# Scan decays from a split sum, and cross attention's products in three rounded parts

## What is computed

```python
# scan: chunks of 128 tokens, 16 heads of 64, 2 groups, state 128
a_cs = jnp.cumsum(ac, axis=-1)
seg = a_cs[..., :, None] - a_cs[..., None, :]
decay = jnp.exp(jnp.where(causal, seg, -jnp.inf))
cb = jnp.einsum('bclgn,bcsgn->bcgls', cm, bm)
y_diag = jnp.einsum('bcgkls,bcsgkp->bclgkp', cb[:, :, :, None] * decay, xc)
decay_to_end = jnp.exp(a_cs[..., -1:] - a_cs)
chunk_decay = jnp.exp(a_cs[..., -1])
def step(h, inp):
    st, dec = inp
    return h * dec[..., None, None] + st, h
y_off = jnp.einsum('bclgn,bcgkpn,bcgkl->bclgkp', cm, prev, jnp.exp(a_cs))

# cross attention: 4 heads of 256, 512 queries, 256 memory tokens
s = jnp.einsum('blhd,bmhd->bhlm', q, k) * (XA_HEAD_DIM ** -0.5)
p = jax.nn.softmax(s, axis=-1)
o = jnp.einsum('bhlm,bmhd->blhd', p, v)
```

## Time and profile before

| | before |
|---|---|
| median of 3 runs | 2520.03 us (2519.97 to 2525.08) |
| the profiled execution's own time | 2524.29 us |
| its span in the profile | 2522.5 us |
| granted clock of TensorE, mean | 0.996 |
| DMA, mean over the span | 100 GB/s |

### The profile page before, as it was taken

How to read it: one execution, slowest core, us unless ns; L and a number is a source line. 1 busy time by engine, 2 the same in 40 slices (tenths; PEclk the granted TensorE clock), 3 DMA queues, 4 the chain that set the end, 5 groups by cost and what they waited for, 6 DMA issues and landing times.

```text
span 2522.5 us, 38409 instructions
## 1 busy us (share of the span) xinstructions
PE 2471.1 (98%) x15181; PEld 2144.2 (85%) x15181; DVE 1699.1 (67%) x3249; ACT 1294.5 (51%) x2558; POOL 404.4 (16%) x476
## 2 busy tenths in 40 slices
PE   7999999999999999999999999999999999999998
PEld 6876677899988978778897999889898887999888
DVE  5476977688863499997774988535635744987533
ACT  4365554367742435564654687424534453677422
POOL 2233342200000156553000100000000100100000
PEclk9999999999999999999999999999999999999999
DMA  9532234434443233223421333332321442333332
GB/s 285 136 93 71 63 101 121 132 99 126 118 126 98 80 101 94 58 67 95 131 84 51 92 111 108 96 96 82 93 76 34 134 126 59 85 111 107 93 99 86
DMA packets 455092, 253.29 MB, mean 100 GB/s; under 512 B 16458, under 2 KB 449310, under 8 KB 454911
## 3 DMA queue, kind: packets, MB, share of 16 engines
q1 hardware_dynamic: 451615, 243.18, 33.7%
q0 software_dynamic: 3152, 7.59, 1.2%
q10 hardware_dynamic: 144, 0.07, 0.0%
HBM read 247.99 MB, written 2.80 MB: 99 GB/s over the span
## 4 chain that ended last, share of the span: by engine, by line
PE 84%; DVE 10%; ACT 3%; issue 2%; DMA 1%; SPq 0%; POOL 0%; DVEq 0%; ACTq 0%; POOLq 0%
PE ps L1134 15%; PE ps L1136 15%; PE ps L1142 15%; PE ps L1199 4%; PE ps L1201 4%; PE ps L1204 4%; PE ps L1049 4%; PE ps L1051 4%; PE ps L1047 4%; PE ps L1375 2%; PE ps L1232 1%; DVE ps L3034 1%; PE ps L1229 1%; PE ps L1227 1%; PE ps L1720 1%
## 5 line engine op out<-in xcount | busy, mean ns | idle before, releaser
L1950 ACT ACTIVATE wh<-w_f 128x512 fp32r<-128x512 f32 (+2 forms) x621 | 351.1, 614 | 337.7 <-PE ps L1142 158.1
L2914 DVE TENSOR_TENSOR w_r<-w_f,wh 128x512 fp32r<-128x512 f32 (+1 forms) x459 | 295.9, 688 | 334.1 <-ACT wh L1950 333.6
L1134 PE MATMUL ps<-XH,wh 128*128 128x512 f32 (+1 forms) x1136 | 458.0, 403 | 4.4 <-ACT wh L1950 3.5
L1136 PE MATMUL ps<-XL,wh 128*128 128x512 f32 (+2 forms) x1016 | 398.0, 392 | 0.2 <-DVE XL L3434 0.2
L1142 PE MATMUL ps<-XH,w_r 128*128 128x512 f32 (+2 forms) x1160 | 309.2, 390 | 1.1 <-DVE w_r L2914 0.8
L1136 PE MATMUL ps<-arena_r,wh 128*128 128x512 f32 (+1 forms) x808 | 297.1, 373 | 0.1
L4213 POOL TENSOR_TENSOR w_r<-w_f,wh 128x256 fp32r<-128x256 f32 (+1 forms) x314 | 236.1, 782 | 352.2 <-ACT wh L1950 352.2
L1134 PEld LDWEIGHTS ps<-XH,wh 128*128 128x128 f32 (+1 forms) x1136 | 211.9, 186 | 69.2 <-issue 16.0
L1142 PEld LDWEIGHTS ps<-XH,w_r 128*128 128x128 f32 (+2 forms) x1160 | 215.5, 186 | 51.2 <-DVE w_r L2914 3.2
L1136 PEld LDWEIGHTS ps<-XL,wh 128*128 128x128 f32 (+2 forms) x1016 | 189.5, 186 | 42.8 <-issue 1.7
L1134 PE MATMUL ps<-arena_r,wh 128*128 128x512 f32 (+1 forms) x568 | 210.6, 379 | 0.8 <-ACT wh L1950 0.8
(11 more groups left out here) (499 smaller groups left out, 5913.4 us busy)
## 6 DMA issues: line engine op xcount, KB each, us to landing
w_f<-in_mlp_w SPq DMA_DIRECT2D x126, 512.0 KB, 4.0
w_f<-in_w_ff SPq DMA_DIRECT2D x63, 512.0 KB, 4.1
w_f<-in_w_in SPq DMA_DIRECT2D x49, 512.0 KB, 3.9
w_f<-in_ada_w SPq DMA_DIRECT2D x35, 512.0 KB, 4.0
w_f<-in_even_w_in SPq DMA_DIRECT2D x35, 512.0 KB, 3.8
w_f<-in_odd_w_in SPq DMA_DIRECT2D x23, 512.0 KB, 3.7
w_f<-in_even_w_out SPq DMA_DIRECT2D x16, 512.0 KB, 3.9
w_f<-in_xa_w_v SPq DMA_DIRECT2D x16, 512.0 KB, 3.3
```

Source lines behind the costliest of these rows:

```text
L1134: e.matmul(b, hi[:, k, :], xh, start=u.first and k == 0, stop=False)
L1136: e.matmul(b, hi[:, k, :], xl, start=False, stop=False)
L1950: e.activation(high_flat(u)[:, s], flat(u, 0)[:, s], ACT.Copy).then_inc(act.sem, act.up("high", u.n, i))
L2914: e.tensor_tensor(low[:, s], raw_[:, s], high[:, s], ALU.subtract).then_inc(dve.sem, dve.up("low", u.n, i))
```

## The change

In the **scan**, the running sums of all 16 heads of a chunk are made in the projections' stage, turned so that heads lie on partitions: three copies of the step widths (`adt_thrice`), four float32 products, a rounded copy of two thirds of the 48 rows and a remainder in the last third, and GpSimd spreads each chunk to 48 x 512 with the other heads set to zero (`decay_split`). A step's seg is then one rounded product of 48 rows by 512 columns. The mask add and its table go: ScalarE takes Relu(a_cs - seg) in four instructions out of PSUM and then one exponential of 128x512 with scale -1; the causal mask is a 0/1 product on C·B that GpSimd does. DE comes from one exponential for all chunks. The old state is multiplied by DE on GpSimd (not in chunk 0, where it is zero). The scan's tap slots change from 3 each (2 in step 14) to 4 in steps 0 to 9 and 3 in 10 to 12; the root's from 4 + 4 to 0 + 3. The first four gated inputs move from step 14 to step 13, and come after that step's outputs.

In **cross attention**, queries, keys, weights and values are split: ScalarE makes the high parts (of keys and values two instructions of 128x1024 each), VectorE the low parts of queries and weights, GpSimd those of keys and values (one instruction of 128x2048 each). Scores and values become three rounded products. The bank of the turned weights and that of a query unit are now freed by VectorE. Some buffers move in the arena.

```diff
         tap_slots |= {("xbc", m): 1 for m in XBC_ORDER[8:XBC_FIRST]} | {("xbc end",): 6}
-        tap_slots |= {("scan", st): 3 if st < 14 else 2 if st == 14 else 0 for st in STEPS}
-        tap_slots |= {("root", 0): 4, ("root", 1): 4}
+        tap_slots |= {("scan", st): 4 if st < 10 else 3 if st < 13 else 0 for st in STEPS}
+        tap_slots |= {("root", 0): 0, ("root", 1): 3}
...
# TensorE
+            for c in range(NT):
+                last = e.matmul(b[0:DECAY_ROWS, c * P:(c + 1) * P],
+                                adt_thrice[:, c * DECAY_ROWS:(c + 1) * DECAY_ROWS],
+                                upper, start=True, stop=True)
...
             def scan_decay(st):
...
-                for j in range(4):
-                    hd = st * 4 + j
-                    last = e.matmul(b[:, j * P:(j + 1) * P], adt[:, hd:hd + 1].to_broadcast([P, P]), upper,
-                                    start=True, stop=True)
+                w.wait_ge(pool, "decay blocks", c)
+                e.matmul(b[:, :], group_pick[0:DECAY_ROWS, q4:q4 + 1].to_broadcast([DECAY_ROWS, P]), decay_split[c],
+                         start=True, stop=True).then_inc(pe.sem, pe.up("seg", st))
...
                 def cross_begin(hd, qt):
-                        last = e.matmul(b[:, 0:MEM], qT[:, 2 * hd + j, qt * P:(qt + 1) * P], kT[:, 2 * hd + j, :],
-                                        start=j == 0, stop=j == 1)
+                        e.matmul(b[:, 0:MEM], q_high[:, m, ts], k_high[:, m, :], start=j == 0, stop=False)
+                        e.matmul(b[:, 0:MEM], q_high[:, m, ts], k_low[:, m, :], start=False, stop=False)
+                        last = e.matmul(b[:, 0:MEM], q_low[:, m, ts], k_high[:, m, :], start=False, stop=j == 1)
...
                 def cross_weigh(hd):
+                    w.wait_ge(dve, "xpt", li, hd, NT - 1)
+                    w.wait_ge(act, "values high", li)
+                    w.wait_ge(pool, "values low", li)
...
-                            last = e.matmul(b[:, :], vv[:, kt, m * P:(m + 1) * P], pt[:, kt, :], start=kt == 0, stop=kt == 1)
+                            e.matmul(b[:, :], v_high[:, kt, c], high[:, kt, :], start=kt == 0, stop=False)
+                            e.matmul(b[:, :], v_high[:, kt, c], low[:, kt, :], start=False, stop=False)
+                            last = e.matmul(b[:, :], v_low[:, kt, c], high[:, kt, :], start=False, stop=kt == 1)
...
# ScalarE, scan_decay: after E1
-                w.wait_ge(dve, "seg", st)
-                w.wait_ge(dve, "nacs")
+                    w.wait_ge(pe, "y", st - 2)
...
-                    e.activation(DEC[:, j, :], DEC[:, j, :], ACT.Exp, bias=nacs[:, hd:hd + 1]).then_inc(
-                        act.sem, act.up("dec", st))
+                    e.activation(DEC[:, j, :], bb[:, j, :], ACT.Relu, bias=acs[:, hd:hd + 1], scale=-1.0).then_inc(
+                        act.sem, act.up("fall", st))
+                att4.free(act, "seg", st)
+                w.wait_ge(act, "fall", st)
+                e.activation(DEC, DEC, ACT.Exp, scale=-1.0).then_inc(act.sem, act.up("dec", st))
...
# VectorE: scan_mask is gone, and in scan_state
-                    e.tensor_tensor(half[par], half[par], de[:, g * 4:(g + 1) * 4, par].unsqueeze(2).to_broadcast([P, 4, DH]),
-                                    ALU.mult).then_inc(dve.sem, dve.up())
...
+                def weights_low(hd, qt):
+                    high, low = (a[:, :, qt * P:(qt + 1) * P] for a in pt_ring[li].of(hd))
+                    w.wait_ge(act, "xpt", li, hd, qt)
+                    e.tensor_tensor(low, att4.of("xt", li, hd, qt)[:, 0:MEM].rearrange("p (a b) -> p a b", a=2),
+                                    high.bitcast(F32), ALU.subtract).then_inc(dve.sem, dve.up("xpt", li, hd, qt))
+                    att4.free(dve, "xt", li, hd, qt)
...
                 for i, tile in enumerate(tiles):
                     cross_begin(*tile)
+                    if i > 1:
+                        weights_low(*tiles[i - 2])
...
# GpSimd, in the loop over st, after CE of st + 1
+                if q4 == 0:
+                    scan_groups(c, 1)
+                elif c < NT - 1 and q4 == 2:
+                    scan_groups(c + 1, 0)
...
+                elif q4 % 2 and 0 < c < NT - 1:
+                    scan_fade(c, q4 // 2)
...
+            def scan_groups(c, g):
+                w.wait_ge(act, "cb", c, g)
+                e.tensor_tensor(CB[:, g, :], CB[:, g, :], upper, ALU.mult).then_inc(pool.sem, pool.up("cb", c, g))
...
+            def scan_fade(c, g):
+                w.wait_ge(pe, "y", 4 * c + 2 * g + 1)
+                w.wait_ge(dve, "state", c - 1, g)
...
+            def values_low(li):
+                w.wait_ge(act, "values high", li)
+                e.tensor_tensor(v_low, vv, v_high.bitcast(F32), ALU.subtract).then_inc(pool.sem, pool.up("values low", li))
```

More of the change, by code:

```diff
@@ L90 @@
 NEAR = 8
+O_KEYS = 12416
+O_PT_LOW = ARENA - 1024 - 16
 ADA_AFTER = {1: 0, 4: 1, 7: 2, 10: 3}
@@ L112, in shape_constants @@
     upper = (i[:, None] <= i[None, :]).astype(np.float32)
-    seg_mask = np.where(i[:, None] <= i[None, :], 0.0, NEG).astype(np.float32)
+    picks = np.zeros((P, PICKS), np.float32)
+    rows = np.concatenate([i[:SSM_HEADS], i[2 * SSM_HEADS:3 * SSM_HEADS]])
+    for j in range(4):
+        picks[rows, j] = rows % 4 == j
+        picks[rows, 4 + j] = rows % SSM_HEADS // 4 == j
     again = np.tile((np.arange(S) % GLA_C != 0).astype(np.float32), (P, 1))
@@ L2102, in evacuate @@
                     lin.free(act, *u.out)
+                elif name in cross_queries:
+                    w.wait_ge(pe, "unit", u.n)
+                    copy(q_high[:, m, :], b, "query high", name[1], m)
                 elif name in TURNED:
@@ L2689, in layer_biases, with keys_high, values_high @@
                 return biases
+            def keys_high(li):
+                for h in range(2):
+                    ks = slice(h * QUARTER, (h + 1) * QUARTER)
+                    w.wait_ge(act, ("mk", li), KC - 1)
+                    copy(k_high[:, ks, :], kT[:, ks, :], "keys high", li)
+            def values_high(li):
+                for t in range(2):
+                    w.wait_ge(act, "stored", ("mv", li), KC - 1)
+                    copy(v_high[:, t, :], vv[:, t, :], "values high", li)
             def cross_attention(stage):
@@ L3064, in evacuate @@
                                            op0=ALU.mult, op1=ALU.add).then_inc(dve.sem, dve.up("yout", m))
+                    lin.free(dve, *u.out)
+                elif name in cross_queries:
+                    w.wait_ge(act, "query high", name[1], m)
+                    e.tensor_tensor(q_low[:, m, :], b[:, :], q_high[:, m, :].bitcast(F32), ALU.subtract).then_inc(
+                        dve.sem, dve.up(name, m))
                     lin.free(dve, *u.out)
@@ L3704, in vector_program @@
                     conv_taps("gv", i)
[L3706 to L3719 removed]
+                if i == 7:
+                    b, low = att4.of("decay rows"), slice(2 * SSM_HEADS, DECAY_ROWS)
+                    w.wait_ge(act, "decay high")
+                    e.tensor_tensor(decay_rows[low, :], b[low, :], decay_rows[low, :].bitcast(F32), ALU.subtract).then_inc(
+                        dve.sem, dve.up("decay low"))
+                    att4.free(dve, "decay rows")
             def scan_decay(st):
@@ L3755, in scan_state @@
             def scan_state(c, g):
-                de = DE.rearrange("p (g two) -> p g two", two=2)
                 b = att4.of("state", c, g)
@@ L3965, in cross_attention @@
                         cross_low((i - 6) // 4)
+                for tile in tiles[-2:]:
+                    weights_low(*tile)
                 cross_low(HEADS - 1)
@@ L4378, in scan_inputs @@
                         pool.sem, pool.up("xw", c, g))
+            def scan_fade(c, g):
+                de = DE[:, c * SSM_HEADS:(c + 1) * SSM_HEADS].rearrange("p (g two) -> p g two", two=2)
+                w.wait_ge(act, "de")
+                w.wait_ge(pe, "y", 4 * c + 2 * g + 1)
+                w.wait_ge(dve, "state", c - 1, g)
+                for par in range(2):
+                    half = pair(ST)[:, g * 4:(g + 1) * 4, par, par * DH:(par + 1) * DH]
+                    e.tensor_tensor(half, half, de[:, g * 4:(g + 1) * 4, par].unsqueeze(2).to_broadcast([P, 4, DH]),
+                                    ALU.mult).then_inc(pool.sem, pool.up("fade", c, g))
             for u in plans["ev xbc"]:
```

146 lines of the change are left out of this document (90 added, 56 removed).

## The result

The changed kernel took 2530.45 us (median of 8 runs, 2528.93 to 2533.28); the kernel before, run beside it, 2526.11 (8 runs, 2519.97 to 2530.99). The ratio is 1.0027, with a 95% interval of 1.0015 to 1.0039: 4 to 10 us slower, where 14.3 us faster was forecast.

A forecast was written before the change was run, and what follows sets the result against it. TensorE, busy 98% of the span, was taken as the bound. Scan -8.1 us and cross attention -6.2 summed to -14.3, from a median of 2520.0 to 2505.7 us; range 2498 to 2517.

The forecast's parts named there:

- VectorE sets the scan: Rival: in the scan VectorE needs 5.59 us a step, so 1.8 us is won instead of 8.6; 2512.5 us, chance 0.14.
- The waits of the values for the weights' low part: Cross attention: TensorE waits for VectorE's subtraction before the values; 2 us a layer, 4 in all (0 to 14).
- 13 x 0.66 = 8.6 us: Scan: one rounded product of 0.23 us replaces sums of 0.89, saving 0.66 a step in 13 steps from seg(3).
- I take that wait as unchanged (0 to 3 us): Scan: ScalarE's evacuation of a finished tile holds up a step, 1.17 us at y(14) before; no change counted.
- -0.4 (0 to 1.4): End of the short convolution: two masks and copies less let VectorE start earlier, saving 0.4 us.
- -11.2: Cross attention: rounded products save 5.8 us on the scores of 32 tiles and 5.4 on the values of eight heads.
- Where a query unit ... lies between, nothing shows: at i = 10.: Cross attention: a query unit of 5.5 us covers the wait for the weights' subtraction, so it costs nothing there.
- I take 1.0, for layer 1 only: Layer 1's cross attention: tile 0's scaling may wait out GpSimd's long instruction on SBUF ports; 1.0 us, range nothing to 3.
- Cross attention gives it back: Rival: the weights' subtraction shows at most tiles, 10 us instead of 5; 2510.7 to 2512 us, chance 0.15.
- its one rival: Scan's loop: ScalarE's chain sets the step, 6.6 us or more; at 7.2 us a step +13, 2533 us; chance 0.04.

The follow-up runs named there:

- e10: Changed kernel with each step's rounded product for the decay sums issued twice; undisturbed steps went from 5.12 to 5.34 and from 5.25 to 5.48 us.
- e9: Changed kernel; in the scan ScalarE evacuates a finished tile behind the next step's decays and GpSimd adds it behind CE; ratio to before 1.0004.
- e7: Changed kernel; in the scan only ScalarE's evacuation of a finished tile moves behind the next step's decays; ratio to before 1.0039.
- e1: Kernel before plus the scan's edits alone, with the old cross attention; ratio to before 1.0006.
- e2: Kernel before plus cross attention's edits alone, with the old scan; ratio to before 1.0040.
- e8: Changed kernel; layer 1's values' parts early, weights' low part behind the query unit, ScalarE's (not GpSimd's) tile-end work late; ratio to before 1.0007.
- e4: Changed kernel with VectorE making the weights' low part of tile i-2 behind the query unit, not ahead of it; ratio to before 1.0023.
- e5: Changed kernel with cross attention's values as float32 products again, scores still three rounded ones; ratio to before 0.9978.
- e3: Changed kernel with layer 1's high and low parts of the values made ahead of the last query unit before cross attention; ratio to before 1.0019.
- e6: Changed kernel with cross attention's scores as float32 products again, values still three rounded ones; ratio to before 1.0035.
- e12: Changed kernel with the old three taps a scan step (2 in step 14), not four in the first ten; ratio to before 1.0030.
- e11: Changed kernel with float32 values, split scores, and ScalarE's and GpSimd's tile-end work in the scan moved later; 2511.99 us, ratio to before 0.9948.

## Why the prediction was wrong, point by point

**What held.** The step of the scan: 5.12 to 5.25 us, 5.1 forecast. VectorE keeps up in the undisturbed steps, about as narrowly as forecast (0.15 us a step to spare): from 1048 to 1080 it stood idle three times, 1.25 us in six steps. C and B's product had a median of 0.71 us, so the rival "VectorE sets the scan" is out. Four Relus took 1.13 to 1.16 us, no table load came, GpSimd was in time in the undisturbed steps. In layer 2 the same lock (a scaling of 4.14 us at 2069.35) cost nothing, as a query unit lay over it. The waits of the values for the weights' low part, set at 4 us for both layers, were 3.7.

**"13 x 0.66 = 8.6 us".** Mis-sized. From the four rounded products ahead of the sums to y it was 0.92 + 0.98 us before and is 1.00 + 0.42: 0.48 saved a step, not 0.66. e10 shows that the product itself was rightly priced; what was missing is 0.09 us ahead of the sums and 0.09 more ahead of y, where weights are loaded late. 13 x 0.18 = 2.3 us.

**"I take that wait as unchanged (0 to 3 us)"**, of a tile's end. It became 2.10 and 1.94 us at two steps, 4.0 in all against 1.2. That is beyond the 3 us of its own bound. ScalarE's and GpSimd's queues had no slack for the work at a tile's end; e9 shows it, and e7 that one queue is not enough. Together: 13 x 0.48 = 6.2 saved, 4.0 lost and 1.2 won back at y(14) make 3.4; measured at full clock, y(2) to y(15) of e1, it is 3.7. The clock's 1.4 us stand against 1.3 in the kernel before and change little in the 4.2 us of the table.

**"-0.4 (0 to 1.4)"**, for an earlier end of the short convolution. It did not show: TensorE's wait there ended at 1041.98, at 1040.75 before, and at 1041.48 in e2, which has the old scan. No run tells what of this is drift.

**"-11.2" for the products of cross attention.** Nearly right. Where no wait disturbs it, a tile with its turning went from 1.08 to 0.94 us and a head's values from 3.43 to 2.72: 32 x 0.14 + 8 x 0.71 = 10.2 us. Between the turnings (14 tiles, 3 heads) that is 4.1 us a layer. But TensorE's busy time fell there by 2.7 us in layer 1 (48.4 to 45.7, e8) and 2.8 in layer 2 (53.6 to 50.7, after), as each wait costs more than its row: the last product ahead of it is not overlapped, and the first behind it starts slowly. In e8's layer 1 that makes 4.1 - 2.7 = 1.4 us for six waits, in layer 2 after 1.3 for five: some 0.24 us a wait, an estimate from these sums. The forecast had no such term.

**"Where a query unit ... lies between, nothing shows: at i = 10."** The step that failed most. I asked what the subtraction waits for and how late that makes the values, and not what stands behind it in VectorE's queue: the roundings, the low part of that very query unit, the next maximum. Three waits of 2.2 to 2.3 us stand behind it (L1754 for L3136 twice, for L2764 once in layer 1); e4 takes 4.8 us back between the turnings, and e5, without the subtraction, has one wait of 0.45.

**"I take 1.0, for layer 1 only"**, of the lock. The mechanism was right, the size wrong: 5.4 us by e3 between the turnings of layer 1, above the 3 that I gave as the end. VectorE's 4.15 us were seen; that three tiles then come late one after the other, and that a clock falls behind them, was not.

**The clock.** Nowhere in the sum. In layer 1 the busy time was 49.85 us against 45.74 in e8 for the same instructions, 4.1 us more; less 0.24 for each of three more waits, some 3.4 are the clock's. So layer 1's +10.1 us are 8.6 of waits + 2.2 at the edges of nine waits + 3.4 of clock - 4.1 of work, and layer 2's +3.2 are 6.1 + 1.2 - 4.1. (The clock's and the edges' parts are worked out from these same windows, so that they add up proves nothing.) In the scan a fall of the clock is chance; here it is not: in all eight executions in which the lock meets tile 0 (after, e2, e4, e6, e7, e9, e10, e12) the clock fell some 10 us behind the start of the scaling; in the six others (before, e1, e3, e5, e8, e11) it did not fall there. The second fall, behind 1358, came in only some of them. The rival "Cross attention gives it back" had 10 us of waits in both layers together; it was 14.7, and gave back more than all.

Why slower got 0.05: its one rival was placed in the scan. Everything that could make cross attention slower than before had been bounded singly (14 us if every tile shows), and 11.2 us of saving stood against it.

## What to carry to other kernels

When a change inserts an instruction that waits for a far-off producer, read the queue behind it: what is ready there and now stands still, and whether the producer's engine needs that itself. Where an engine has been full without a gap, a stall is not worth its own length but that, its edges (0.24 us each here) and the slow clock that may follow. And price a replaced product by the start-to-start time of the block with its neighbours, not by its own record.

## What was not expected of the hardware

- Under a GpSimd instruction of 4.6 us on SBUF, VectorE's scaling of an SBUF row (128x256, float32, one tensor) stood until it ended. It took 4.14 or 4.15 us in all eighteen cases in which it began within 0.7 us of GpSimd's start (eight in layer 1, ten in layer 2), and 0.99 and 0.98 in the two in which it began later (layer 1 of e3 and e8); in all twenty it ended 0.15 us after GpSimd's instruction. Instructions with an operand in PSUM (0.69, 0.41 us) and single-column ones (0.15 to 0.17) ran at their usual time. The Trainium skill (SBUF — State Buffer, "Who interferes with whom") names two-input SBUF instructions and two-port modes; the first kind is not this one, the second may be. No run here tells which mode the scaling has.
- Stalls of 0.53 and 1.41 us in the scan were followed by half clock in four executions and not in two others of the same order; the waits at the lock (in the changed kernel four of 0.61 to 2.34 us within 7 us) were followed by it in eight of eight.
- A wait of TensorE costs some 0.24 us more than the idle time in its row, an estimate from e8 and after.
- Between the rounded product of the sums and y's first product TensorE's starts lie 0.42 us apart, 0.19 more than between two rounded ones, though elsewhere a rounded product is followed by a float32 one after 0.23: at y the weights are loaded with the product, elsewhere under the one before.
